# Mixture-of-experts layer of a decoder trunk: rows of a group resident on the chip, chosen and placed by one-hot products, one norm per group

## The reference

```python
def route(xf, w_router, b_router):
    s = jax.nn.sigmoid((xf @ w_router).astype(jnp.float32))
    sel = s + b_router.astype(jnp.float32)
    grp = jnp.sum(lax.top_k(sel.reshape(-1, N_EXPERT_GROUPS, EXPERTS_PER_GROUP), 2)[0], -1)
    g_best = jnp.argmax(grp, axis=-1)
    in_grp = (jnp.arange(N_EXPERTS) // EXPERTS_PER_GROUP)[None, :] == g_best[:, None]
    _, e_idx = lax.top_k(jnp.where(in_grp, sel, NEG_INF), TOP_K)
    w = jnp.take_along_axis(s, e_idx, axis=-1)
    return e_idx, w / jnp.sum(w, -1, keepdims=True)
...
    def expert_block(args):
        xb, e = args
        h = jax.nn.silu(xb @ w_gate[e]) * (xb @ w_up[e])
        return h @ w_down[e]
...
        x = layer_norm(DEEPNORM_ALPHA * x + y.reshape(B, S, D), ln_g[l, 2], ln_b[l, 2])
```

## Time and profile before

| | us |
|---|---|
| median of 3 runs | 1112.08 |
| lowest and highest run | 1108.95, 1112.49 |
| span of the profiled execution, first to last instruction | 1106.8 |
| TensorE matmul busy | 1033.0 |
| VectorE busy | 343.2 |
| ScalarE busy | 251.5 |
| GpSimd busy | 101.6 |
| bytes moved by DMA | 265.73 MB, mean 240 GB/s |

### The profile page before, as it was taken

The page is one execution under the profiler, slowest core; times in us unless marked ns, Lnnn a source line. Parts: engine busy times, 40 slices in busy tenths (PEclk is TensorE's granted clock), DMA queues, the critical chain, the costliest instruction groups (busy, mean ns, idle before and its releaser), DMA issues.

```text
span 1106.8 us, 15722 instructions
## 1 busy us (share of the span) xinstructions
PE 1033.0 (93%) x6596; PEld 516.4 (47%) x6596; DVE 343.2 (31%) x724; ACT 251.5 (23%) x510; POOL 101.6 (9%) x141
## 2 busy tenths in 40 slices
PE   8999999999898999999999999999999999887896
PEld 4444455557655554566544733333333333333342
DVE  0179623234655645203215511111111111011015
ACT  2341122234435520013401111111111111011023
POOL 2000100000000000100000211111111111110123
PEclk9999999999999999999999999999999999999999
DMA  8012320211222150553833899999999999999995
GB/s 274 23 65 76 115 77 2 78 43 51 63 77 80 76 191 1 181 236 113 311 121 121 341 417 419 423 419 418 419 416 422 415 423 414 416 417 408 417 415 210
DMA packets 57462, 265.73 MB, mean 240 GB/s; under 512 B 7122, under 2 KB 8274, under 8 KB 32560
## 3 DMA queue, kind: packets, MB, share of 16 engines
q1 hardware_dynamic: 51200, 255.49, 58.2%
q0 software_dynamic: 4960, 8.15, 2.0%
q10 hardware_dynamic: 1232, 1.08, 0.3%
HBM read 256.56 MB, written 16.25 MB: 246 GB/s over the span
## 4 chain that ended last, share of the span: by engine, by line
PE 34%; DMA 20%; DVE 3%; ACT 1%; issue 1%; DVEq 0%; SPq 0%; ACTq 0%
PE cpair L2051 7%; DMA ring<-in_w_exp_up 7%; PE bank L2061 6%; DMA xT<-in_w_exp_up 4%; DMA ring<-in_w_exp_down 4%; PE tpair L2051 4%; DMA keys<-in_w_exp_up 3%; DMA ar<-in_w_exp_down 3%; PE bank L1890 2%; PE bank L1870 2%; PE tpair L1890 1%; PE bank L1863 1%; PE cpair L1890 1%; PE tpair L1870 1%; PE cpair L1870 1%; PE bank L2033 1%
## 5 line engine op out<-in xcount | busy, mean ns | idle before, releaser
L2051 PE MATMUL cpair<-ring,xgT 128*64 128x512 f32 x344 | 115.0, 598 | 6.4 <-DMA xT<-in_w_exp_up 4.1
L2491 DVE TENSOR_TENSOR hs<-cpair,hs 64x512 f32<-64x512 f32 x21 | 14.5, 693 | 252.4 <-ACT hs L2273 252.4
L2273 ACT ACTIVATE hs<-cpair 64x512 f32<-64x512 f32 x21 | 12.4, 588 | 235.5 <-PE cpair L2051 235.5
L2051 PEld LDWEIGHTS cpair<-ring,xgT 128*64 128x64 f32 x344 | 36.0, 138 | 58.4 <-issue 58.4
L1793 POOL DMA_INDIRECT y_rows<-ye,tabs x30 | 30.5, 1018 | 352.2 <-ACT xgt L2279 331.3
L922 PE MATMUL bank<-xT,ring 128*128 128x512 f32 x128 | 60.9, 606 | 0.0
L2051 PE MATMUL tpair<-ring,xgT 128*64 128x512 f32 x168 | 56.5, 593 | 0.0
L365 PE MATMUL bank<-xT,ring 128*128 128x512 f32 x112 | 48.5, 593 | 0.0
L2491 DVE TENSOR_TENSOR hs<-tpair,hs 64x512 f32<-64x512 f32 x11 | 7.6, 693 | 125.5 <-ACT hs L2273 125.5
L941 PE MATMUL tpair<-ring,mixT 128*128 128x512 f32 x96 | 42.0, 594 | 0.0
L2061 PE MATMUL bank<-ring,hT 128*64 128x512 f32 x128 | 32.4, 653 | 4.1 <-DVE hT L2495 4.1
(11 more groups left out here) (479 smaller groups left out, 1913.5 us busy)
## 6 DMA issues: line engine op xcount, KB each, us to landing
ring<-in_w_exp_up SPq DMA_DIRECT2D x32, 1024.0 KB, 10.2
ring<-in_w_exp_gate SPq DMA_DIRECT2D x32, 1024.0 KB, 10.4
ring<-in_w_exp_down SPq DMA_DIRECT2D x16, 1024.0 KB, 10.6
ring<-in_w_in SPq DMA_DIRECT2D x6, 2048.0 KB, 8.1
ring<-in_w_mem_kv SPq DMA_DIRECT2D x4, 2048.0 KB, 10.3
opening<-in_w_exp_gate SPq DMA_DIRECT2D x8, 1024.0 KB, 10.3
mixT<-in_w_exp_down SPq DMA_DIRECT2D x8, 1024.0 KB, 10.5
mixT<-in_w_exp_gate SPq DMA_DIRECT2D x8, 1024.0 KB, 10.4
```

The costliest lines, as they stand in the source:

```text
L2051: last = nc.tensor.matmul(bank[b][m * CAP:(m + 1) * CAP, :], xgT[:, j, h, :], w(m, h)[:, j * DE:(j + 1) * DE], start=(k == 0), stop=(k == ...
L2491: V.tensor_tensor(hb, bank[1 + e % 3][CAP:P, :], sil, ALU.mult).then_inc(h_done, 1)
```

## The change

Two things are changed, in the last stage alone.

1. **Resident groups.** POOL gathers the rows of a whole group (up to 128 tokens, whole rows of 4 KB) into one of two buffers `xgt`, 8 gathers in place of 32. Out of it, TensorE picks the rows of two experts at once with a one-hot matrix (`select` on VectorE, `chosen(p)` on TensorE: eight f32 products with the rows as stationary operand, already turned), and the transposes of `tokens` go. The down output is copied by ScalarE (`rows_read`) and placed into the group's rows by a second one-hot matrix that holds the gates (`placing` on VectorE, `placing_turned`, `combined` on TensorE), summed over the four experts in two PSUM banks. Then the group is added to `ALPHA` times its rows, normed (`finished`, `deviation`, `root`) and scattered straight to the output. `y_rows`, its clearing and reading back, and the closing norm of four tiles are gone; `ln3` is loaded by DMA, early. Routing has other steps: group ranks and token numbers first, then expert ranks and one table. `UNREAD` has other counts. One place of 1 MB is given up (23 left). The overflow path is new: it applies when a group has over 128 or an expert over 64 tokens.
2. **Order.** The last two experts are made as the others: gate and up, then down.

Cut to what the working speaks of:

```diff
-UNREAD = (26, 6, 10, 3)
+UNREAD = (20, 5, 10, 4, 14)
...
-        products = [(e, kind, h) for e in range(LAST - 1) for kind in (GU, DN) for h in range(2)]
-        products += [(e, kind, h) for kind in (GU, DN) for e in (LAST - 1, LAST) for h in range(2)]
+        products = []
+        for e in range(NE):
+            products += [(e, GU, h) for h in range(2)]
+            products += [(e, DN, h) for h in range(2)]
...
-                    for n in range(7):
+                    for h, src in enumerate((ln_g, ln_b)):
+                        sp.dma_start(ln3[:, h, :], src[0, 2:3, :].to_broadcast([P, D])).then_inc(ln3_here, 16)
+                    for n in range(6):
...
-                    sp.wait_ge(comb_done, 1)
+                    sp.wait_ge(more_known, 1)
...
+                    def gather(g):
+                        return pool.indirect_dma_start(xgt[:, g % 2, :], None, xs_rows[:, :],
+                                                       bass.IndirectOffsetOnAxis(gtok[:, g:g + 1].bitcast(U32), 0),
+                                                       bounds_check=rows_end, oob_is_err=False)
+                    def scatter(g):
+                        return pool.indirect_dma_start(out_v[:, :], bass.IndirectOffsetOnAxis(gtok[:, g:g + 1].bitcast(U32), 0),
+                                                       xgt[:, g % 2, :], None, bounds_check=rows_end, oob_is_err=False)
 
                     pool.wait_ge(lg_full, 2)
...
                     pool.wait_ge(xs_out, 64)
                     pool.wait_ge(tokens_known, 1)
-                    pool.indirect_dma_start(xg[:, 0, :], None, xs_halves[:, :],
-                                            bass.IndirectOffsetOnAxis(tabs[:, 0, 0:1].bitcast(U32), 0),
-                                            bounds_check=limit, oob_is_err=False).then_inc(xg_here[0], 16)
+                    gather(0).then_inc(xg_here[0], 16)
                     pool.tensor_tensor(blkones[:, 15:16], blkones[:, 14:15], blkones[:, 14:15], ALU.add).then_inc(asked, 1)
...
+                    gather(1).then_inc(xg_here[1], 16)
+                    for g in range(NGRP):
+                        pool.wait_ge(rows_done, g + 1)
+                        scatter(g).then_inc(out_rows[g % 2], 16)
+                        if g + 2 < NGRP:
+                            pool.wait_ge(out_rows[g % 2], 16 * (g // 2 + 1))
+                            gather(g + 2).then_inc(xg_here[g % 2], 16)
...
+                    def ranks(dst, hot, width):
+                        nc.tensor.matmul(dst[:, 0:NT * width], before[:, :], hot, start=True, stop=False)
+                        for n in range(1, NT):
+                            last = nc.tensor.matmul(dst[:, n * width:NT * width], ones[:, :], hot[:, 0:NT - n, :],
+                                                    start=False, stop=(n == NT - 1))
+                        return last
...
+                    pe.wait_ge(gsel_done, 1)
+                    ranks(bank[4], gsel, NGRP).then_inc(ranks_full, 1)
+                    nc.tensor.matmul(bank[6][:, 256:256 + NT * NGRP], ones[:, :], gsel, start=True, stop=True)
                     unread(UNREAD[1])
                     pe.wait_ge(ids_done, 1)
-                    token_columns(pe, ls, 0)
-                    nc.tensor.matmul(bank[5][:, 0:P], ones[:, :], both_k, start=True, stop=True).then_inc(rk_full, 1)
+                    pe.wait_ge(hits_done, 1)
+                    for t in range(NT):
+                        last = nc.tensor.matmul(bank[6][:, 0:NGRP], hit[:, t, :], tok_of[:, t, :],
+                                                start=(t == 0), stop=(t == NT - 1))
+                    last.then_inc(tokens_full, 1)
                     unread(UNREAD[2])
-                    pe.wait_ge(ids_done, 2)
-                    pe.wait_ge(gates_done, 1)
-                    row_and_gate_columns(pe, ls)
+                    pe.wait_ge(oh_done, 1)
+                    ranks(bank[5], oh[:, :, :], NE).then_inc(ranks_full, 1)
+                    nc.tensor.matmul(bank[7][:, 256:256 + P], ones[:, :], oh[:, :, :], start=True, stop=True)
                     unread(UNREAD[3])
+                    pe.wait_ge(vals_done, 2)
+                    for t in range(NT):
+                        last = nc.tensor.matmul(bank[7][:, 0:2 * NE], hit[:, t, :], vals[:, t, :, :].rearrange("p f e -> p (f e)"),
+                                                start=(t == 0), stop=(t == NT - 1))
+                    last.then_inc(table_full, 1)
+                    unread(UNREAD[4])
...
+                    def chosen(p):
+                        g = 2 * p // EPG
+                        pe.wait_ge(sel_done, 2 * p + 2)
+                        pe.wait_ge(xg_here[g % 2], 16 * (g // 2 + 1))
+                        if p:
+                            pe.wait_ge(x_read, 2 * p)
+                        for h in range(2):
+                            for k in range(KT // 2):
+                                last = nc.tensor.matmul(tpair[:, h, k * P:(k + 1) * P],
+                                                        xgt[:, g % 2, h * 512 + k:(h + 1) * 512:KT // 2],
+                                                        sel[:, :, :].rearrange("p e c -> p (e c)"), start=True, stop=True)
+                            last.then_inc(x_full, 1)
...
+                    def placing_turned(e):
+                        pe.wait_ge(selg_done, e + 1)
+                        if e:
+                            pe.wait_ge(comb_read, e)
+                        nc.tensor.transpose(bank[4][:, 256 + e % 2 * P:256 + (e % 2 + 1) * P], selg[:, e % 2, :], ident[:, :])\
+                            .then_inc(comb_full, 1)
...
+                    def combined(e):
+                        i, g = e % EPG, e // EPG
+                        pe.wait_ge(y_read, e + 1)
+                        pe.wait_ge(comb_read, e + 1)
+                        if i == 0 and g:
+                            pe.wait_ge(square_done, 2 * g)
+                        for h in range(2):
+                            last = nc.tensor.matmul(bank[6 + h][:, :], combT[half[h], e % 2, :], ye[half[h], e % 2, :],
+                                                    start=(i == 0), stop=(i == EPG - 1))
+                        last.then_inc(c_done, 1)
+                    chosen(0)
+                    for e in range(NE):
                         gate_up(e, 0)
                         gate_up(e, 1)
...
+                        if e:
+                            combined(e - 1)
+                        if e % 2 and e < LAST:
+                            chosen((e + 1) // 2)
+                        placing_turned(e)
+                        hidden(e)
+                        down(e)
+                    combined(LAST)
...
+                    def chosen(p):
+                        if p:
+                            act.wait_ge(w_read, read_at[2 * p - 1, GU, 1])
+                        for h in range(2):
+                            act.wait_ge(x_full, 2 * p + h + 1)
+                            nc.scalar.activation(xgT[:, 4 * h:4 * h + 4, :, :].rearrange("p k e c -> p (k e c)"), tpair[:, h, :],
+                                                 ACT.Copy).then_inc(x_read, 1)
...
+                    def rows_read(e):
+                        act.wait_ge(w_read, read_at[e, DN, 1])
                         if e >= 2:
...
+                            act.wait_ge(c_done, e - 1)
+                        nc.scalar.activation(ye[:, e % 2, :], bank[5][:, :], ACT.Copy).then_inc(y_read, 1)
...
+                    def deviation(g):
+                        act.wait_ge(mean_done, g + 1)
+                        act.wait_ge(set_done, 5)
+                        for h in range(2):
+                            nc.scalar.activation(bank[6 + h][:, :], xgt[:, g % 2, h * 512:(h + 1) * 512], ACT.Square,
+                                                 bias=nmean[:, :], accum_out=total[:, 2 + h:3 + h]).then_inc(square_done, 1)
+                    def root(g):
+                        act.wait_ge(added, 2 * g + 2)
+                        act.wait_ge(rooted, 2 * g + 1)
+                        nc.scalar.activation(rstd[:, 0:1], rstd[:, 0:1], ACT.Sqrt, bias=eps[:, :], scale=1.0 / D)\
+                            .then_inc(rooted, 1)
+                    chosen(0)
+                    for e in range(NE):
+                        silu(e)
+                        if e % 2 and e < LAST:
+                            chosen((e + 1) // 2)
+                        if e and e % EPG == 0:
+                            deviation(e // EPG - 1)
+                            root(e // EPG - 1)
+                        rows_read(e)
+                    deviation(NGRP - 1)
+                    root(NGRP - 1)
...
+                    dve.wait_ge(ranks_full, 1)
+                    own_rank = g8[:, 3, :, :]
+                    link(dve, V.tensor_tensor(own_rank, gsel, bank[4][:, 0:NT * NGRP].rearrange("p (t g) -> p t g", t=NT), ALU.mult))
```

(57 more changed lines are left out.)

834 lines of the change are left out of this document (290 added, 544 removed).

## The result

The changed kernel takes 1137.84 us (median of 4 runs, 1136.97 to 1138.93) against 1110.51 us before (median of 4 runs): ratio 1.0253, 95% interval 1.0236 to 1.027. It is 27 us slower; 5.5 were forecast, and 1132 was the end of the range.

A forecast was written before the change was run, and what follows sets the result against it. DMA bounds the kernel now, TensorE after the change. Start 631.25 + cycles 431.0 + choice 26.4 + clock 8.5 + 0.2 + end 13.3 = 1110.7 us span, plus 5.3 gives 1116.0 us; range for 8 in 10: 1104 to 1132.

The forecast's parts named there:

- gate and up of expert 0 begins: Start of the experts on TensorE: at 631.25 us against 629.94 before, +1.3 us.
- 32 cycles of 13.47: TensorE's pass through the experts at the old cycle of 13.47 us: 431.0 us.
- choice behind odd experts: chosen on TensorE delays the hidden transposes by 1.76 us behind 15 odd experts: 26.4 us.
- falls of the clock: Granted clock halves for about 3.4 us, one per 96 us, 5 in 466 us: 8.5 us.
- end: Closing work behind the last down product: 13.3 us against 19.7, -6.4; bounds 12 and 17.
- the term of `chosen`: Sixteen TensorE instructions at 0.116 us take 1.86 us, behind every odd expert but the last.
- rival B: chosen's operand, read with a stride of four, costs 0.17 us an instruction: +13 us, 1129; chance 0.17.
- B's own test: A TensorE cycle of 16 us or more behind odd experts means that B holds.
- the bound moved from DMA to TensorE: Expert stage: TensorE is through at 1088 us, DMA at 1066, so TensorE no longer catches up.
- the norm hidden: A group's norm on VectorE takes about 8 us; TensorE needs VectorE after 11.1, 3 us to spare.
- the table load of SiLU out of the way: ScalarE's SiLU behind a root pays nothing for its table load; otherwise 7 x 1.28 = 9 us.
- the full drain: TensorE array-shape changes cost 0.10 us, not the full drain's 0.17, which would add 2 us in all.

The follow-up runs named there:

- run on the hidden rows: Changed kernel, but VectorE writes the product of expert rows so that TensorE's transposes of the hidden rows read neighbouring columns: 1132.17 us, ratio to before 1.0187.
- run with neighbouring columns: Changed kernel, but chosen takes 128 neighbouring columns of the gathered rows as stationary operand instead of every fourth: 1102.62 us, ratio to before 0.9929.
- the kernel before with the hidden-rows edit: Kernel before the change, with VectorE writing the product of expert rows in the order in which TensorE turns them: 1108.9 us, ratio 0.9998.

## Why the prediction was wrong

By its own terms, against the span forecast at 1110.7 and measured at 1135.1 (+24.4):

| term | forecast | measured | off by |
|---|---|---|---|
| gate and up of expert 0 begins | 631.25 | 635.45 | +4.2 |
| 32 cycles of 13.47 | 431.0 | 431.0 | 0 |
| choice behind odd experts | 15 x 1.76 = 26.4 | 15 x 3.61 = 54.2 | +27.8 |
| falls of the clock | 8.5 | 1.5 | -7.0 |
| end | 13.3 | 12.8 | -0.5 |

The rows sum to +24.5 (a term of 0.2 in the forecast's sum has no row). From the span to the median I added 5.3; it is 2.7 here, -2.6, which leaves the miss of 21.8 us.

**The step that failed** is the term of `chosen`. It took 0.116 us an instruction from the filling products, whose operand lies in neighbouring columns, for an operand with a stride of four. The only row with this form stood in the prediction, as rival B: two f32 products with such an operand, 0.34 us. I put it aside with "the first of a kind is always slow". In the kernel before, all 64 of these loads are as slow as those of `chosen` (L2033 reads the tokens' rows at a stride of four):

```profile
L2033 PEld LDWEIGHTS tpair<-ident,xgt 128*128 128x128 f32 x64 | 17.4, 320 | 24.4 <-issue 24.4
```

Neighbouring columns bring loads of this size to 191 ns. The run on the hidden rows shows the same for another pair that opens its group: its two loads fall from 315 to 184 ns and are still the first of their kind. So it was the stride and not the beginning; on L2033 itself the stride was never taken away. B's own test, a cycle of 16 or more behind odd experts, is met with 17.08, and B is the case that came; its price was too low as well (0.17 an instruction, from a pair; 0.245 with sixteen in a row), and by its own terms 2.72 is 0.77 over 1.95, not 0.89. Without the stride the term would have held: 15 x 1.66 = 24.9 us in the run with neighbouring columns, against 26.4.

**Right**: the bound moved from DMA to TensorE, and the last piece of weights, issued as the second of the row below at 1068.8 and landed at 1079.6, lies ready 40 us before TensorE reads it (I had given 1056 for the issue; the pace of 2.56 us a piece is the forecast one, but the first of these pieces goes out at 639.15, and I let pieces land 5 us after their release where it takes 10); `combined` 1.06 us, as summed with the change of array shape (0.97 + 0.09); DMA's bytes; the even cycle unchanged; the norm hidden (3.8 us to spare by the trace, 3 forecast); the table load of SiLU out of the way; the end at 12.8. The change of shape behind `combined` cost 0.09; by the full drain that the Trainium skill (TensorEngine Tiling (Array Packing), Key Properties) speaks of, at the 0.17 of the prediction, it would be 1.14 instead of 1.06.

```profile
1066.33 2.82 SPq L1437 DMA_DIRECT2D ring<-in_w_exp_down  x2
```

**The beginning** was 4.2 late. chosen(0) starts 16.12 us after the first filling product (16.6 forecast). I let gate and up begin 1.9 us behind it, after chosen's first half and its copy; in truth both halves stand in front of it in TensorE's queue. Without the stride that would have been the same (1.88 with neighbouring columns), with it it is 3.82: 1.4 us in all, and the same cause as above. The other 2.8 were there before any changed step: the last addition on VectorE ahead of routing runs at 607.70, against 604.91 in the profile before, and the granted clock had fallen at 455 to 465 us in the one and not in the other (windows with the granted clock third from the right; after, then before):

```profile
455.00:465.00 10.00, 9.22 (x24) 5.54 (x25) 4.20 (x7) 1.24 (x3) 5.04 (x18) 0.66 0.85 283
```

```profile
455.00:465.00 10.00, 8.99 (x33) 5.66 (x34) 4.25 (x7) 1.23 (x3) 5.09 (x15) 1.00 0.84 281
```

The two profiles are still level at the table load of 394 us (393.89 after, 394.12 before) and 2.8 apart at the next, 507.77 and 504.99. In eleven other profiles this addition stands between 604.61 and 609.33. Whether the changed order of the early loads plays a part was not tested and stays open.

**The clock** was priced at one fall per 96 us, the distance between the first two falls of the kernel before; its six falls would have given one per 80 or so. The changed kernel had one between 640 and 1122 us, +1.5 us in its cycle, and its variants in which TensorE is the bound had none to three; the kernel before with the hidden-rows edit had eight. Two falls are too few for a rate. Why the changed kernel has fewer is not shown.

**The order** of the last two experts was given no cost: it is 1.5 us, and stands in the 32 full cycles, since the kernel before has two waits less at its end.

## What to carry to other kernels

Price an instruction by a row with the same operand, stride and partitions, and where the only such row is dear, let it carry the sum until something explains it away. Work that is moved into a wait costs the full excess over the wait as soon as the engine becomes the bound, so it pays to spread it over all waits of the cycle, and to count how far the next bound is: here some 40 of the 54 us were to be had. A control that is to tell two bounds apart has to be priced in its own kernel first: the hidden-rows edit was worth 0.40 us behind a covered hole and 0.05 behind an open one, too little to tell.

## What the runs showed of the hardware

- Loads of a 128 x 128 f32 stationary operand for two-pass products: 191 ns at a stride of 1 element, 196 at 2, 328 at 4, 334 at 8; spacing of such instructions 0.12, 0.13, 0.245 and 0.25 us. With 64 rows: 184 at stride 1, 315 at 4.
- Single-pass transposes suffer less. With 128 columns streamed past the operand a load takes 190 ns at a stride of 8 elements (L1869) against 141 unstrided (L868), and both follow each other at 0.11 us, so that the stride costs nothing. With 64 rows and 64 columns (the hidden rows, L1960) it does: 260 ns and 0.11 us apart at a stride of 4, 157 ns and 0.06 us apart in the run on the hidden rows.
- VectorE pays 1032 ns instead of 693 for a product of 64 x 512 elements written in scattered order (steps of 512 bytes), and 0.63 us for a copy of 128 x 512 read at a stride of four.
- Whether the load of an activation table stands ahead of its instruction's wait differs. The root's comes behind the sum that it needs, in every group (1127.63 in the last, 1.28 us on its path); the SiLU's comes ahead (636.18 for expert 0, whose SiLU ran at 642.59; 712.96 behind a root, for 717.14), so it cost nothing.
